# Streaming encoder trunk on one core: the next product's first two weight units in two passes around the third tile's norm

## What is computed

```python
for i in range(DEPTH):                      # DEPTH = 4
    m = mixer[i % 3](x, ...)                # fox, hgrn, pool
    x = layer_norm(ALPHA * x + m, ln_g[i, 0], ln_b[i, 0])
    x = layer_norm(ALPHA * x + swiglu_ffn(x, w_ffn_in[i], w_ffn_out[i]), ln_g[i, 1], ln_b[i, 1])
```

## Time and profile before

| | us |
|---|---|
| runs of the kernel before, median of 3 | 2037.82 |
| lowest, highest | 2030.97, 2039.06 |
| the profiled execution's own time | 2038.09 |
| its span, first to last instruction | 2036.2 |
| TensorE busy in the span | 1921.4 |
| VectorE, ScalarE, GpSimd busy | 970.4, 709.9, 219.1 |

### The profile page before, as it was taken

The page is one execution under the profiler, slowest core; times in us unless marked ns, Lnnn a source line. Parts: engine busy times, 40 slices in busy tenths (PEclk is TensorE's granted clock), DMA queues, the critical chain, the costliest instruction groups (busy, mean ns, idle before and its releaser), DMA issues.

```text
span 2036.2 us, 29670 instructions
## 1 busy us (share of the span) xinstructions
PE 1921.4 (94%) x12360; PEld 1738.4 (85%) x12360; DVE 970.4 (48%) x1509; ACT 709.9 (35%) x1119; POOL 219.1 (11%) x358
## 2 busy tenths in 40 slices
PE   5998999999989999899999969999999899999997
PEld 5988879998877887689998869998888788899985
DVE  3355464333455677644333664333543455533433
ACT  3235423333245435233332233333232453333321
POOL 4003200000061213130000100000030130000000
PEclk8899999999989999899999979999989999999998
DMA  6245434443343333254433324433353462444431
GB/s 215 91 145 194 138 115 127 131 126 124 114 146 95 108 117 98 70 157 124 125 126 124 125 93 124 124 125 124 117 187 105 166 203 78 142 127 124 127 128 66
DMA packets 179156, 259.43 MB, mean 127 GB/s; under 512 B 14669, under 2 KB 122333, under 8 KB 179024
## 3 DMA queue, kind: packets, MB, share of 16 engines
q1 hardware_dynamic: 160736, 195.61, 30.1%
q0 software_dynamic: 18288, 61.94, 9.5%
HBM read 243.20 MB, written 13.19 MB: 126 GB/s over the span
## 4 chain that ended last, share of the span: by engine, by line
PE 87%; DVE 6%; ACT 3%; DMA 2%; issue 1%; POOL 1%; SPq 0%; ACTq 0%; DVEq 0%; POOLq 0%
PE ps L1438 15%; PE ps L1439 14%; PE ps L1440 14%; PE ps L1447 10%; PE ps L1449 10%; PE ps L1448 10%; PE ps L1626 1%; PE ps L1702 1%; PE ps L1613 1%; DVE xT_lo L683 1%; DVE x_tok L737 1%; DMA w_raw<-in_w_fox_in_dram 1%; DVE x_tok L722 1%; PE ps L1685 1%; DVE stats L711 1%
## 5 line engine op out<-in xcount | busy, mean ns | idle before, releaser
L664 DVE TENSOR_TENSOR w_lo<-w_raw,w_hi 128x1024 fp32r<-128x1024 f32 x370 | 456.9, 1239 | 813.4 <-ACT w_hi L385 812.9
L385 ACT ACTIVATE w_hi<-w_raw 128x1024 fp32r<-128x1024 f32 x370 | 389.9, 1059 | 922.0 <-DMA w_raw<-in_w_ffn_in_dram 408.3
L1438 PE MATMUL ps<-xT_hi,w_hi 128*128 128x384 f32 x1664 | 570.5, 343 | 23.3 <-DVE xT_lo L683 22.3
L1439 PE MATMUL ps<-xT_lo,w_hi 128*128 128x384 f32 x1664 | 568.7, 342 | 0.0
L1440 PE MATMUL ps<-xT_hi,w_lo 128*128 128x384 f32 x1664 | 568.6, 342 | 0.0
L1438 PEld LDWEIGHTS ps<-xT_hi,w_hi 128*128 128x128 f32 x1664 | 318.8, 192 | 26.3 <-issue 24.6
L1439 PEld LDWEIGHTS ps<-xT_lo,w_hi 128*128 128x128 f32 x1664 | 318.8, 192 | 0.3
L1440 PEld LDWEIGHTS ps<-xT_hi,w_lo 128*128 128x128 f32 x1664 | 318.3, 191 | 0.0
L1449 PE MATMUL ps<-w_hi,hT_lo 128*128 128x512 f32 x528 | 209.6, 397 | 0.0
L1447 PE MATMUL ps<-w_hi,hT_hi 128*128 128x512 f32 x528 | 209.2, 396 | 0.0
L1448 PE MATMUL ps<-w_lo,hT_hi 128*128 128x512 f32 x528 | 207.7, 393 | 0.0
(11 more groups left out here) (295 smaller groups left out, 1995.2 us busy)
## 6 DMA issues: line engine op xcount, KB each, us to landing
w_raw<-in_w_ffn_in_dram SPq DMA_DIRECT2D x352, 256.0 KB, 3.2
w_raw<-in_w_ffn_out_dram SPq DMA_DIRECT2D x176, 256.0 KB, 2.8
w_raw<-in_w_fox_in_dram SPq DMA_DIRECT2D x96, 256.0 KB, 2.9
k_c<-in_cache_fox_k_dram POOLq DMA_DIRECT2D x32, 512.0 KB, 4.7
v_c<-in_cache_fox_v_dram POOLq DMA_DIRECT2D x32, 512.0 KB, 3.8
w_raw<-in_w_hgrn_in_dram SPq DMA_DIRECT2D x64, 256.0 KB, 3.0
w_raw<-in_w_fox_out_dram SPq DMA_DIRECT2D x32, 256.0 KB, 2.7
gb<-in_ln_g_dram POOLq DMA_DIRECT2D x8, 512.0 KB, 4.0
```

What stands on the lines that cost most here:

```text
L385: nc.scalar.activation(w_hi[:, slot, :], w_raw[:, slot, :], ACT.Copy).then_inc(hi_ready, 1)
L664: V.tensor_tensor(w_lo[:, slot, :], w_raw[:, slot, :], w_hi[:, slot, :].bitcast(F32), ALU.subtract).then_inc(lo_ready, 1)
L1438: mm(out, w_hi[:, slot, cols], x_hi[:, k, :], start=k == 0, stop=False)
L1439: mm(out, w_hi[:, slot, cols], x_lo[:, k, :], start=False, stop=False)
```

## The change

At the six norms that hand over to plain transposes (`PAIRED`):

- TensorE transposes the first half of tile 1 before the last six matmuls of tile 2's tail, the second half after the tail (`turn_half`, with the waits of `free`).
- `first_pair` takes the place of the first two `unit_fm`. Its first pass runs both units over tiles 0 and 1, 48 matmuls of 256 columns; the second runs them over tile 2, 48 matmuls of 128 columns. The two halves of tile 2 are transposed inside the first pass: one before its last 12 matmuls, one after them. The first pass waits for tile 1's first split, the second for tile 2's first, the third unit for all six.
- VectorE splits both halves of tile 0 and the first of tile 1 before tile 2's residual, and (2, first), (1, second), (2, second) after tile 2's norm. ScalarE rounds both halves of tile 1 before scale 2.
- The transposes get other banks, away from those that `first_pair` writes; two of them wait for an earlier split (`LO_TURN`).
- In the pool layer VectorE normalises tile 0 before it splits tile 2 of the averages, and the four `w_hi` of norm 3's freed slots move on ScalarE from before scale 0 of norm 4 to after it.

```diff
@@ -302,11 +302,15 @@
+        PAIRED = [n for n in range(1, 2 * DEPTH) if n not in AVERAGED]
+        LO_TURN = {(0, 0): 1, (0, 1): 2, (1, 0): 3, (2, 0): 4, (1, 1): 5, (2, 1): 6}
...
+            if n == 0 or n in AVERAGED:
+                bank = (0, 1, 2, 3, 7, 4)[2 * t + hf]
+            else:
+                bank = 4 * ((n + 1) % 2) + (0, 3, 1, 0, 2, 3)[2 * t + hf]
...
@@ -412,12 +416,18 @@
                 rstd_of(n, 0)
-                for t in range(1, NTOK):
-                    rstd_of(n, t)
-                    if n < LN_LAST:
-                        transposed_tile(n + 1, t - 1)
+                if n in AVERAGED:
+                    last_w_hi(START[n // 2 - 1]["down"], CF)
+                rstd_of(n, 1)
                 if n < LN_LAST:
-                    transposed_tile(n + 1, NTOK - 1)
+                    transposed_tile(n + 1, 0)
+                if n + 1 in PAIRED:
+                    transposed_tile(n + 1, 1)
+                rstd_of(n, 2)
...
@@ -756,12 +771,13 @@
-                    if turn and t:
+                    if n + 1 in AVERAGED and t:
                         split_tile(n + 1, t - 1)
+                    if turn and n + 1 in PAIRED:
+                        for tt, hf in ((), ((0, 0), (0, 1), (1, 0)), ((2, 0), (1, 1), (2, 1)))[t]:
+                            split_half(n + 1, tt, hf)
                 if n + 1 in AVERAGED:
                     return
-                if turn:
-                    split_tile(n + 1, NTOK - 1)
...
@@ -1059,21 +1075,22 @@
                 residuals(0)
+                normalise_tile(n, 0)
                 split_tile(n, 2)
-                normalise_tile(n, 0)
-                w_lo_of(out0 + 2)
...
@@ -1456,15 +1474,57 @@
+            def free(n, t, hf):
+
+                pe.wait_ge(*at(LN[n - 1]["x"], 2 * t + hf + 1))
+                if (t, hf) == (1, 1):
+                    pe.wait_ge(*at(TR[n]["lo"], LO_TURN[0, 0]))
+                if (t, hf) == (2, 1):
+                    pe.wait_ge(*at(TR[n]["lo"], LO_TURN[0, 1]))
+
+            def first_pair(n, m, bank0):
+
+                lo = TR[n]["lo"]
+                if n - 1 in AVERAGED:
+                    pe.wait_ge(*at(LN[n - 1]["resid"], 5))
+                for t0, t1, after in ((0, 2, (1, 0)), (2, 3, (2, 0))):
+                    tt = slice(t0 * P, t1 * P)
+                    pe.wait_ge(*at(lo, LO_TURN[after]))
+                    for u in range(2):
+                        slot = (m + u) % RING
+                        if t0 == 0:
+                            pe.wait_ge(lo_ready, m + u + 1)
+                        for kk in range(2):
+                            k = 2 * u + kk
+                            if t0 == 0 and k == 3:
+                                turn_half(n, 2, 0, lambda t, hf: free(n, t, hf))
+                            for b in range(4):
...
+                        if t0:
+                            last.then_inc(unit_used, 1)
+                    if t0 == 0:
+                        turn_half(n, 2, 1, lambda t, hf: free(n, t, hf))
+                pe.wait_ge(*at(lo, 6))
...
+                            if t == NTOK - 1 and n < LN_LAST and v == TAIL - 1 and kk == 0 and n + 1 in PAIRED:
+                                turn_half(n + 1, 1, 0, normed(n))
...
-                if n < LN_LAST and n + 1 not in AVERAGED:
-                    for t in range(1, NTOK):
-                        turn_tile(n + 1, t, normed(n))
+                if n < LN_LAST and n + 1 in PAIRED:
+                    turn_half(n + 1, 1, 1, lambda t, hf: free(n + 1, t, hf))
...
+                    if c == 0:
+                        first_pair(2 * i + 1, s["up"], 4)
+                    for u in range(0 if c else 2, CU):
+                        unit_fm(s["up"] + CU * c + u, u, 4 * ((c + 1) % 2), xT_hi, xT_lo)
```

More of the change, by code:

```diff
@@ L1437, in unit_fm @@
                         out = ps[:, bank0 + n, 0:T]
[L1438 to L1440 removed]
+                        mm(out, w_hi[:, slot, cols], x_hi[:, k, :], start=k == 0, stop=False, skip_group_check=True)
+                        mm(out, w_hi[:, slot, cols], x_lo[:, k, :], start=False, stop=False, skip_group_check=True)
+                        last = mm(out, w_lo[:, slot, cols], x_hi[:, k, :], start=False, stop=k == KD - 1,
+                                  skip_group_check=True)
                 last.then_inc(unit_used, 1)
@@ L1457, in unit_tm, with turn_half @@
                 last.then_inc(unit_used, 1)
+            def turn_half(n, t, hf, ready):
+                bank, out = turned(n, t, hf)
+                ready(t, hf)
+                for k in range(4):
+                    c = (4 * hf + k) * P
+                    ins = nc.tensor.transpose(out[:, k, :], x_tok[:, t, c:c + P], ident[:, :])
+                ins.then_inc(TR[n]["done"][0], 1)
             def turn_tile(n, t, ready):
                 for hf in range(2):
-                    bank, out = turned(n, t, hf)
@@ L1463, in turn_tile @@
-                    ready(t, hf)
-                    for k in range(4):
-                        c = (4 * hf + k) * P
-                        ins = nc.tensor.transpose(out[:, k, :], x_tok[:, t, c:c + P], ident[:, :])
-                    ins.then_inc(TR[n]["done"][0], 1)
+                    turn_half(n, t, hf, ready)
+            def free(n, t, hf):
[4 more added lines that the diff above has]
+                    pe.wait_ge(*at(TR[n]["lo"], LO_TURN[0, 1]))
@@ new lines, in first_pair @@
+            def first_pair(n, m, bank0):
[14 more added lines that the diff above has]
+                            for b in range(4):
+                                cols = slice(kk * WCOLS + b * P, kk * WCOLS + (b + 1) * P)
+                                out = ps[:, bank0 + b, tt]
+                                mm(out, w_hi[:, slot, cols], xT_hi[:, k, tt], start=t0 == 0 and k == 0, stop=False,
+                                   skip_group_check=True)
+                                mm(out, w_hi[:, slot, cols], xT_lo[:, k, tt], start=False, stop=False, skip_group_check=True)
+                                last = mm(out, w_lo[:, slot, cols], xT_hi[:, k, tt], start=False, stop=False,
+                                          skip_group_check=True)
+                        if t0:
[3 more added lines that the diff above has]
+                pe.wait_ge(*at(lo, 6))
@@ L1915, in pool @@
                 product(2)
-                for t in range(NTOK):
-                    if t == 1:
-                        pe.wait_ge(*at(LN[n]["resid"], 5))
-                    turn_tile(n + 1, t, normed(n))
+                for t in range(2):
+                    for hf in range(2):
+                        turn_half(n + 1, t, hf, lambda t, hf: free(n + 1, t, hf))
             pe.wait_ge(ident_ready, 2)
```

45 lines of the change are left out of this document (27 added, 18 removed).

## The result

The changed kernel took **2001.55 us** (median of 4 runs, 2000.34 to 2004.45) against 2036.08 for the kernel before on the same chip: a ratio of **0.9835** with a 95% interval of 0.9811 to 0.9859. Two later timings of the same kernel (after2 and after3, under Experiments) have medians of 2005.95 and 2006.11 us and ratios of 0.9856 and 0.9874: they lie just inside it, and the third gain, some 26 us, is as large as forecast. The two profiled executions looked at here differ by more than the medians: spans of 1998.7 and 2036.2 us, so 37.5 us to be explained where the forecast has 26.2.

A forecast was written before the change was run, and what follows sets the result against it. TensorE was taken as the bound, its idle time and half clock at the handovers to be won: 22.9 us at five handovers plus 5.5 in the pool layer minus 2.2 for masks, 26.2 us, so 2012 us, range 2005 to 2024.

The forecast's parts named there:

- The five handovers: Tail's end to third unit outside the pool layer: 13.3 us each in place of 17.59 to 18.20, 22.9 us won.
- the 0.3 us for semaphores: In each handover's path: waits for semaphores take 0.3 us over the whole handover.
- VectorE's slack: First half of tile 2 ready before the first pass's 36th matmul: 0.5 us spare at norm 1, 0.1 to 0.3 at norm 0.
- The price of a narrow matmul: Second pass: 128-column matmuls start every 0.11 us, so 48 take 5.3 us; ends 0.058 and 0.11.
- The pool layer: Handover at the pool layer: pair starts at 1184.3, third unit at 1198.6 in place of 1204.16, 5.5 us won.
- This starts about 1.5 us earlier: Pool layer: tile 2's residual on VectorE starts about 1.5 us earlier, after scale 0 comes 3.7 us earlier.
- So it costs nothing.: Slots freed in the second pass, the first 1.4 us later against the third unit's start: no cost for units six ahead.
- The masks: After norm 1: GpSimd's masks ready at 609.3, TensorE there at 607.1, so minus 2.2 us; bounds nothing and 4 us.
- The dropped clock in the narrow pass: Rival: the second pass halves the clock, 7.6 us lost at each of six handovers, 2058 us; 5%.
- The slipping chain: Rival: VectorE and ScalarE bring tile 2's first half 2 us late each time, 2024 to 2028 us; 14%.
- the change without effect: Rival: a wait left in place holds the pair back until tile 2 is through, 2038 us; 2%.
- More than forecast: Rival: masks in time and half the narrow pass hidden, masks alone 2010, 8%; narrow matmuls at 0.058 us, 1997, 3%.

The follow-up runs named there:

- no_pair: The changed kernel with the pair undone: TensorE transposes tile 2, waits for all six splits, runs both units over all 384 tokens; 2040.96 us, ratio 1.0044.
- parts: The changed kernel with GpSimd's state loads after the masks, small masks last, and sum masks rounded in two parts; 1994.82 us, ratio 0.9827.
- filler: The kernel before, with 14 useless 512-column matmuls between the transposes of tiles 1 and 2 at five of six handovers; 2018.19 us, ratio 0.9930.
- narrow3: The changed kernel with the pair in three passes of 128 columns, one for each tile; 2041.47 us, ratio 1.0039.

## Why the prediction was wrong in its size, and what in it held

**The step that failed.** The sum has two costs at a handover, the idle time and the half clock behind it, and lets the second end when the clock is back, at 580.81 in the earlier trace rows; for the feed-forward blocks behind it the sum has nothing. In the first profile of the kernel before it goes on: in two blocks of 1008 matmuls the distance stays at 0.1767 us instead of 0.1733 to the block's end, 6.7 us, and these are gone with the change. They are the largest part of what the measurement has above the forecast. Without them the profile would show 30.8 us saved, which is 2007 us and inside the range. By how much this counts in a timing is chance: it was two, two and three blocks in the three profiles of the kernel before.

**What bounds the kernel.** Right. The idle time and half clock of the earlier trace rows were most of what there was to win; no_pair, with both back, is no faster than before.

**The five handovers: 22.9 us forecast, 25.0 measured.** The two large terms held: 36 matmuls of 256 columns took 4.35 us (4.3), the second pass 5.39 (5.3), so the earlier trace rows priced both widths well. What was too large are small terms of the sum. Four transposes in a row with matmuls take 0.36 us and not 0.5, three times in the path (in the tail 0.49): I had halved the 1.04 us that eight show in the earlier trace rows, which is a duration and not a distance between starts. And the 0.3 us for semaphores did not appear. VectorE's slack sufficed: tile 2's first half is scaled in time at all five.

**The price of a narrow matmul.** 0.112 us, as the earlier trace rows had it. The 81 ns that the Trainium skill gives (TensorE: Matmul & The Clock Gate, Back-to-back issue gap) would have made the second pass 3.9 us; the trace has 5.39.

**The pool layer: 5.5 forecast, 6.8 measured.** "This starts about 1.5 us earlier" was too small: tile 2's residual starts 2.0 us earlier (18.1 us behind the averages of tile 2, before 20.1), and the terms behind it, 8.2 and 0.7 us, held. So the pair began 9.4 us earlier and not 9.0, and took 13.5 us to the third unit and not 14.3.

**"So it costs nothing."** This failed. I looked for what the later release of the first unit's slot would delay and found nothing; what mattered was that the third unit now starts 9 us earlier than before, 5.7 of them against the state loads of GpSimd, which are issued from 571.7 on (before from 575.0). The weights six units ahead landed 7.9 us behind the third unit where it had been 0.6, and TensorE's idle time before its first 512-column unit grew from 2.55 to 5.45 us.

**The masks: minus 2.2 forecast.** The wait is there and of that kind, and is larger: the first sum comes 6.2 us late. Two terms of this part were mis-sized. The handover is 5.7 us shorter and not 4.7. And the sum let GpSimd's chain only start 0.65 us later and kept its length; it started no later behind the tail's end (5.4 us in both) but took 38.9 us instead of 35.2, from its first instruction at 570.17 (before 573.38) to the copy's end at 609.05 (before 608.60). The selects of `row_m` and `bd` alone took 3.0 us more. parts shows 7.3 us to be had from late weights and late masks.

That the stretch to norm 2 lost only 1.7 us, where the term says 2.2, is luck: the kernel before lost some 6 us at the stretch's end. There the clock fell in the rests ahead of the output product, and in the changed kernel's first profile it did not. filler, which has the first sum at 25.8 us as before and no fall there either, takes 273.10 us, so like for like the change loses 8.2 us here. (First before, then changed, each a window of a rest and one behind it:)

```profile
833.60:837.60 4.00, 2.69 (x3) 0.86 (x4) 1.92 (x9) 1.58 (x8) 0.00 (x0) 0.50 0.00 0
841.60:845.60 4.00, 4.00 (x11) 3.13 (x10) 0.00 (x0) 0.00 (x0) 0.00 (x0) 0.50 0.44 131
```
```profile
830.90:834.90 4.00, 2.51 (x11) 0.87 (x7) 2.76 (x12) 1.61 (x8) 0.00 (x0) 1.00 0.00 0
838.90:842.90 4.00, 4.00 (x19) 3.20 (x18) 1.88 (x3) 0.00 (x0) 0.00 (x0) 1.00 0.16 34
```

The rests are alike. Over three profiles each the stretch took 279.6, 279.5 and 283.1 us before and 281.8, 282.1 and 286.3 with the change: in the last of these the clock fell there too. What decides was not settled. narrow3 adds a lesson: from norm 1's tail end to norm 2's it takes 288.9 us, the changed kernel 294.1, although narrow3's handover is 5.0 us longer: its first sum comes 26.4 us behind the third unit, not 32.0, and the half clock takes 6.8 us of the stretch, not 20.5.

**The 11.3 us above the forecast.** They are 6.7 us of matmul spacing, 2.1 of the handovers, 1.3 of the pool layer, and 1.3 of the recurrence and all else.

**The rivals.** The dropped clock in the narrow pass did not come about, and narrow3 shows that it could have, had narrow matmuls alone stood behind the pool layer's rest. The slipping chain and the change without effect are out by the windows. "More than forecast" is what happened, but not by its two mechanisms: the masks were later and narrow matmuls as dear as assumed.

## What to carry to other kernels

Look for the stretch where the bound engine waits on one tile's norm, and give it the part of the next product that needs the other tiles: 48 matmuls more paid for themselves because they fell into a rest that had also cost the clock. Put the wider pass first, since in these runs a stream of 128-column matmuls kept whatever clock it found. But do not count the shorter handover as won before looking at the next stage: some 8 us were lost again in the recurrence, against a run whose masks were in time. When a stage is moved 9 us forward, list every queue that was timed against its old place (here a load on GpSimd's queue and the masks it builds), and cut the work that others wait for into the part that they need first.

## What was not expected of the hardware

- A stream of 384-column matmuls in which the clock returned had, in 12 of 26 cases, a distance of 0.1767 us instead of 0.1733 until the block's end, 3.4 us for each block; with the clock at 1.00 from the first matmul it was 0.1733 in all 38.
- 144 matmuls of 128 columns, back to back from an idle stretch on, ran 32.31 us at 0.50 without the clock rising; the same stream behind dense work stayed at 1.00 for 17.29 us.
- Fourteen matmuls that compute nothing, put into each of five rests of some 3.4 us, made the kernel 0.7% faster.
- A GpSimd select on 8 columns took 1.07 to 1.27 us beside VectorE's `w_lo`, and two of them 0.45 us beside a split with one input in PSUM.
